# A weight strip's low part made by GpSimd in four operations of 512 columns in place of one of 2048

## The reference

```
h = _rmsnorm(x, norm_w[layer])
proj = jnp.einsum('bsd,de->bse', h, w_in[layer])
...
merged = (jax.nn.sigmoid(ma_raw) * jnp.einsum('bsw,wd->bsd', y_a, w_proj_a[layer])
          + jax.nn.sigmoid(mb_raw) * jnp.einsum('bsw,wd->bsd', y_b, w_proj_b[layer]))
x = x + jnp.einsum('bsd,de->bse', merged, w_out[layer])
```

## Time and profile before

| | |
|---|---|
| median of three runs | 1780.12 us |
| profiled execution | 1774.67 us |
| its span | 1772.9 us |
| TensorE matmul busy | 1632.1 us (92%) |
| VectorE busy | 762.5 us (43%) |
| ScalarE busy | 630.6 us (36%) |
| GpSimd busy | 480.9 us (27%), 237 instructions |
| of which L1089, 85 operations | 367.3 us |
| mean granted clock of TensorE | 0.961 |

### The profile page before, as it was taken

One profiled execution on the slowest core, in us unless ns is written; L12 is line 12 of the kernel. 1 busy time (PEld: TensorE's weight loads), 2 busy tenths in 40 slices (PEclk: granted clock), 3 DMA queues, 4 the chain that ended last, 5 costly groups with the idle time before them and its releaser, 6 DMA issues.

```text
span 1772.9 us, 23041 instructions
## 1 busy us (share of the span) xinstructions
PE 1632.1 (92%) x9320; PEld 1298.5 (73%) x9320; DVE 762.5 (43%) x1302; ACT 630.6 (36%) x1014; POOL 480.9 (27%) x237
## 2 busy tenths in 40 slices
PE   5999989899999979999799998999998899999996
PEld 5888888798877757777588897655586775555565
DVE  2346266265375331011368611666614434444424
ACT  5322312312312322212443122666623424555632
POOL 3332222213112353333532232333332230010221
PEclk9999999899999979999899999999998999999998
DMA  5231212302233334333321121000021120000101
GB/s 182 93 119 48 94 51 72 96 24 72 72 96 96 95 119 166 118 120 117 131 72 61 59 79 48 18 19 19 1 63 48 59 60 10 10 18 25 48 25 48
DMA packets 129315, 122.75 MB, mean 69 GB/s; under 512 B 11348, under 2 KB 125152, under 8 KB 129216
## 3 DMA queue, kind: packets, MB, share of 16 engines
q1 hardware_dynamic: 129216, 121.33, 21.8%
HBM read 116.87 MB, written 2.10 MB: 67 GB/s over the span
## 4 chain that ended last, share of the span: by engine, by line
PE 65%; issue 13%; DVE 10%; POOL 6%; ACT 3%; DMA 2%; SPq 1%; DVEq 0%; POOLq 0%; ACTq 0%
PE ps L1944 6%; PE ps L1945 5%; PE ps L1946 5%; PE ps L1990 5%; POOL w_lo L1089 5%; PE ps L2424 3%; PE ps L2403 3%; PE ps L2413 3%; PE ps L2153 2%; PE ps L2152 2%; PE ps L2154 2%; PE ps L2255 2%; PE ps L2246 2%; PE ps L2018 2%; PE ps L2404 2%
## 5 line engine op out<-in xcount | busy, mean ns | idle before, releaser
L1089 POOL TENSOR_TENSOR w_lo<-raw,w_hi 128x2048 fp32r<-128x2048 f32 (+2 forms) x85 | 367.3, 4323 | 863.0 <-ACT w_hi L649 784.4
L1944 PE MATMUL ps<-h_hi,w_hi 128*128 128x512 f32 x632 | 262.4, 415 | 21.9 <-issue 5.7
L1945 PE MATMUL ps<-h_lo,w_hi 128*128 128x512 f32 x632 | 255.0, 403 | 0.0
L1946 PE MATMUL ps<-h_hi,w_lo 128*128 128x512 f32 x632 | 254.6, 403 | 0.0
L649 ACT ACTIVATE w_hi<-raw 128x2048 fp32r<-128x2048 f32 (+1 forms) x77 | 145.4, 1888 | 271.2 <-DMA raw<-in_w_in_dram 84.3
L1944 PEld LDWEIGHTS ps<-h_hi,w_hi 128*128 128x128 f32 x632 | 124.6, 197 | 54.6 <-issue 17.8
L1946 PEld LDWEIGHTS ps<-h_hi,w_lo 128*128 128x128 f32 x632 | 123.9, 196 | 28.0
L1945 PEld LDWEIGHTS ps<-h_lo,w_hi 128*128 128x128 f32 x632 | 124.6, 197 | 24.8
L1990 PE MATMUL ps<-qf,kf 128*128 128x64 f32 x448 | 87.6, 277 | 7.1 <-DVE tot_b L1319 6.1
L1037 ACT ACTIVATE pT_b<-ps 128x512 f32<-128x512 f32 x96 | 56.9, 594 | 94.3 <-PE ps L2413 93.1
L1990 PE MATMUL ps<-qb,kb 128*128 128x64 f32 x448 | 88.3, 279 | 0.0
(11 more groups left out here) (441 smaller groups left out, 3485.6 us busy)
## 6 DMA issues: line engine op xcount, KB each, us to landing
raw<-in_w_in_dram SPq DMA_DIRECT2D x32, 1024.0 KB
raw<-in_ada_w_dram SPq DMA_DIRECT2D x24, 1024.0 KB
raw<-in_a_w_in_dram SPq DMA_DIRECT2D x10, 1024.0 KB
raw<-in_w_in_dram SPq DMA_DIRECT2D x16, 512.0 KB
raw<-in_b_w_in_dram SPq DMA_DIRECT2D x5, 1024.0 KB
raw<-in_w_proj_a_dram SPq DMA_DIRECT2D x4, 1024.0 KB
raw<-in_w_proj_b_dram SPq DMA_DIRECT2D x4, 1024.0 KB
raw<-in_w_out_dram SPq DMA_DIRECT2D x4, 1024.0 KB
```

What stands on the lines that cost most here:

```text
L1089: nc.gpsimd.tensor_tensor(w_lo[:, ph.w(s), c], raw[:, s % 2, c], w_hi[:, ph.w(s), c].bitcast(F32), ALU.subtract).then_inc(s_lo, 1)
L1944: mm(ps[:, j, :], wh[:, k, c], xh[:, k, :], start=(k == 0), stop=False)
L1945: mm(ps[:, j, :], wh[:, k, c], xl[:, k, :], start=False, stop=False)
L1946: last = mm(ps[:, j, :], wl[:, k, c], xh[:, k, :], start=False, stop=(k == KT - 1))
```

## The change

In `lo` the one subtraction becomes a loop over pieces of `S` = 512 columns, and only the last piece raises `s_lo`. A strip of 2048 columns is made in four operations; the two strips of 1024 columns in two, the eight of 768 in two (512 and 256). The first strip (L1095 to L1098) has code of its own and stays as it was: two halves of 1024 columns.

```
--- before.py
+++ after.py
@@ -1086,8 +1086,11 @@
             def lo(ph, it, s, c=slice(0, 2 * D)):
 
                 pool.wait_ge(s_hi, ph.k(it, s) + 1)
-                nc.gpsimd.tensor_tensor(w_lo[:, ph.w(s), c], raw[:, s % 2, c], w_hi[:, ph.w(s), c].bitcast(F32),
-                                        ALU.subtract).then_inc(s_lo, 1)
+                for a in range(c.start, c.stop, S):
+                    p = slice(a, min(a + S, c.stop))
+                    last = nc.gpsimd.tensor_tensor(w_lo[:, ph.w(s), p], raw[:, s % 2, p], w_hi[:, ph.w(s), p].bitcast(F32),
+                                                   ALU.subtract)
+                last.then_inc(s_lo, 1)
```

## The result

The kernel after takes 1764.8 us (median of 7 runs, 1753.5 to 1768.8) where the kernel before, run beside it, takes 1774.8 us (7 runs, 1768.9 to 1781.1). The ratio is 0.9930, with a 95% interval of 0.9903 to 0.9956, so the change makes the kernel about 12 us faster by the ratio (8 to 17) and 10 us by the two medians. The two profiled executions, after and before, stand at 1765.18 us (span 1763.4, mean granted clock 0.964) and 1774.67 us (0.961): 9.5 us apart.

A forecast was written before the change was run, and what follows sets the result against it. TensorE, busy 92% of the span, bounds the kernel, with waits for strips and for VectorE operations that strips hold up. Terms -13.7 + 3.2 + 0.5 - 2.5 = -12.5 us: 1762.2 profiled, 1768 on the median's scale; range 1757 to 1781.

The forecast's parts named there:

- Price of a strip, 0.4 us: Each 2048-column strip: four operations take 4.97 us to the last's end against 4.55 for one, plus 0.4 us.
- Where it is paid, +3.2: Seven direct TensorE waits for w_lo grow 0.4 us each, 2.8, and the wait for g_lat by 0.4.
- 485 and the gates, -7.4: L1477 gets in earlier: gain 1.9 us of the 2.7 wait behind 485.38, and 5.5 at the two ada waits.
- x_sq, -1.6: L1561 at 918.41 ends 2.0 us earlier, so TensorE's 1.6 us wait for x_sq goes.
- x_st -0.9, e_st -1.9, vb -1.0: L1602, L1741 and L1807 get in earlier: x_st's 0.9 us wait goes, e_st's 3.5 loses 1.9, vb's 2.4 about 1.0.
- f_g, -0.9: L1870 at 1730.68 ends 3.2 us earlier, but a projection must wait for the strip until 1735.8: gain 0.9 us.
- The chains, +0.5, taking turns: L1316 chains (qf, kf, qb, kb, tot): VectorE and GpSimd alternate at joints, nothing won, 0.5 us lost over all.
- The rival that VectorE keeps the port: VectorE holds the port through a chain, gaining 7.1 us more: -21.6 us, 1758 us; chance 0.14.
- The clock, -2.5: Shorter waits spare some half-clock stretches behind the 2.7 us wait and ada waits: between 0 and 10 us, taken as 2.5.
- given back nearby: Rival: TensorE comes earlier to unlisted waits, half of 13.7 gained, no clock gain: -3.2 us, 1777 us; chance 0.20.
- The slower rival: The port doesn't open inside a strip, so strips hold VectorE 4.95 us, not 4.55: +9.7 us, 1790 us; chance 0.09.

The follow-up runs named there:

- second job: Four kernels, the kernel after with other piece sizes: 1536 + 512 ratio 0.9960, 1024 x 2 0.9940, 512 + 1536 0.9938, 256 x 8 0.9975.
- the fused kernel: Kernel before, strips whole, with L1477 and L1478 made one VectorE operation that takes one input from PSUM: 1766.5 us, ratio 0.9949.
- the heads alone: Pieces of 512 columns only in the heads phase, other strips whole as in the kernel before: 1771.4 us, ratio 0.9991.
- merge only: Pieces of 512 columns only for strips made inside the merge loop, others whole as in the kernel before: 1778.8 us, ratio 1.0031.
- gates only: Pieces only for strips made during the gates phase, others whole as in the kernel before: 1766.8 us, ratio 0.9973.

## Why the prediction was right, and where its steps were not

The forecast was 12.5 us off the profiled time of before, and 1768 us on the median's scale. Measured were 1764.8 us, 9.5 us less in the profiles and 12 by the ratio. The sum is near, but its parts aren't: forecast were 10.0 us less idle time and 2.5 by the clock, and the profiles have 7.1 less idle time, 3.6 by the clock and 1.2 us more work at full clock. The mechanism is shown: the joint lets VectorE in (second job), the operations seen to be held read and write SBUF alone, and one with an input from PSUM isn't (the fused kernel), and no opening was seen inside one operation. By its terms:

- **Price of a strip, 0.4 us.** Right: 0.14 for each of three more operations, 0.42.
- **Where it is paid, +3.2.** Right for the places named: six of the seven waits for w_lo grew by 0.40 to 0.52 us each, as priced, one fell by 0.43, and that for g_lat grew by 0.5, 2.8 in all. The waits for w_lo grew by 4.4 because two are new. The one of 1.20 us at 76.74 cost next to nothing: TensorE had waited there for kb_new, 1.16 us, behind a VectorE operation held for 3.97 us. That wait, which the list of gains lacked, is the one that went, and the strip that had been done 0.8 us before its use came last in its place. The one of 1.00 us at 620.55 (behind the L1480 of the timeline above) isn't a strip that was nearly late: before, TensorE came to this strip 3.7 us after it was done, held by its 4.00 us for ada. It is a part of that gain given back, for which the prediction took 0.3.
- **485 and the gates, -7.4.** This is the step that failed, though the time came out. From the first L1477 to TensorE's start behind yb_lo it is 166.9 us before and 161.3 after, 5.6 less; but of that idle time is only 0.7 (19.3 to 18.7), and half clock 5.5 (12.1 to 6.6). The first gains came as forecast: the wait of 2.71 us behind 485 is 0.73 (1.98 less, 1.9 forecast), and those for ada fell by 5.8. Then they were given back: the next wait for tot_b, 0.51 us at 519.49, is 1.82, yb_lo took 3.8, and the new wait for w_lo 1.0. With whole strips and the fused operation that tot_b wait is 1.52 us and the one for yb_lo 7.7, so this is no price of the pieces: TensorE comes earlier to what it must wait for anyway. The prediction took back 1.1 us here. That the clock gave nearly as much as the idle time should have is luck.
- **x_sq, -1.6.** Wrong; nothing was gained. The step freed one operation, L1561, but it heads a chain of four that share the port. From the start of the earlier trace rows's L1561 to the end of the chain it was 4.94 us (918.41 to 923.35), and it is 4.77 now, with a piece before two of the four. My own reading of the chains of L1316 was not applied here:

```profile
915.01 0.73 DVE L1564 TENSOR_TENSOR x_sq<-x_sq,tmp 128x512 f32<-128x512 f32 x1
915.66 1.77 DVE L1565 SCALAR_TENSOR_TENSOR x_sq<-tmp,fw,x_sq 128x512 f32<-128x512 f32 x1
917.54 1.58 DVE L1564 TENSOR_TENSOR x_sq<-x_sq,tmp 128x512 f32<-128x512 f32 x1
919.04 0.74 DVE L1565 SCALAR_TENSOR_TENSOR x_sq<-tmp,fw,x_sq 128x512 f32<-128x512 f32 x1
```

- **x_st -0.9, e_st -1.9, vb -1.0.** Right: gone, 3.5 to 1.7, 2.6 to 1.5.
- **f_g, -0.9.** Mis-sized: the wait fell by 3.0. I held that the projection of the earlier trace rows must wait for its strip to 1735.8. It is a projection of the strip before, whose low part was long there; after, TensorE goes on at 1727.28, while the new strip is made until 1729.26:

```profile
1723.23 6.03 POOL L1091 TENSOR_TENSOR w_lo<-raw,w_hi 128x512 fp32r<-128x512 f32 x4 [6.81 <-ACT w_hi L649]
1724.23 0.82 DVE L1873 TENSOR_TENSOR f_sum<-f_sum,tmp 128x512 f32<-128x512 f32 x1 [13.62 <-ACT tmp L1074]
...
1727.28 0.78 PE L1947 MATMUL ps<-b_hi,w_hi 128*128 128x512 f32 x1
```

- **The chains, +0.5, taking turns.** Right: kb and tot_a are 0.5 us longer, and the tot_b waits other than the two of the bullet on the gates differ by 0.13 us at most. The rival that VectorE keeps the port (1758 us) is ruled out by the heads alone.
- **The clock, -2.5.** The total, -3.6, is near, but by luck. By part it is -3.6, -6.3, +6.1 and +0.2, and the prediction put nothing on the merge phase; the first -3.6 lies in a part that scatters by more than that (last section). Over the kernels that were run, the half clock costs 2.7 to 7.0 us in the merge phase with whole strips (eight kernels with before), 2.7 to 8.3 with two pieces, 7.5 and 8.8 with four, 9.5 with eight. So four and eight pieces lie above every kernel with whole strips, and two pieces can't be told from them; what decides a single case isn't settled.

The rival "given back nearby" (1777) holds in the gates phase, where it took nearly all of the idle time, and at x_sq. Behind the merge phase the gains stayed (6.6 us less idle time), so its total is ruled out: it wants 3 us, and the interval begins at 8. The slower rival is ruled out.

## What to carry to other kernels

Look at what a long operation on one engine holds up on another: here a 128x4 operation took 4.5 us. Cut it where its neighbour comes, not everywhere: each joint costs 0.14 us, an operation that waits leaves at the next joint, and a chain of them gains nothing. Where a waiting operation can take an input from PSUM in place of SBUF, no cut is needed, and that was worth more in its phase: 195.0 and 195.6 us in two kernels with whole strips there, 201.5 to 202.5 in three with four pieces, 205.5 to 209.4 in three with neither. By the ratio of the whole kernel (0.9949 against 0.9973 for pieces in the gates phase alone) the two aren't told apart. Price a cut in each phase by itself, with the clock behind the waits that it lengthens, and follow a gain to the next thing that the engine waits for.

## What the runs showed of the hardware

- A GpSimd operation of this kind with no semaphore step between it and the next still hands over the port at its joint (L1480 ended 0.28 or 0.29 us behind the next joint or the strip's end, at both places near 615 and 635 us, in every kernel that has it), and in a chain the two engines get it in turn (1.78 us for each of kf, qb and kb).
- Stretches of half clock make one profiled execution a poor witness for a phase. Up to the first L1477, the four kernels with the same whole strips (before, merge only, gates only, fused) took 485.4, 479.2, 480.4 and 491.4 us, with 18.0, 11.4, 13.3 and 23.1 us lost to half clock. The 2.4 us of that part in the first table are within this, and the ratio of the heads alone, 0.9991, says so too.
- The price of waits in the merge loop showed mostly in the clock: 0.6 us more of idle time and 6.1 us more of half-clock loss in the same phase (1.3 and 4.8 with pieces in that loop alone). In one profile each: with whole strips that loss alone scatters from 2.7 to 7.0 us.
